# Output projection's weights and first heads loaded and split during attention's last phase

## The reference

```
hx = rms_norm(x, g_pre) * (1 + scale_x) + shift_x
q, k, v, gate = mla_qkv(hx, ...)                     # 8 heads, 192-wide q and k, 128-wide v
ox = softmax(q k^T / sqrt(192)) v                     # keys: 2048 latent + 256 context
yx = (ox * silu(gate)) @ w_o                          # 1024 x 1024, the output projection
x  = x + gate_x * rms_norm(yx, g_post)
```

## Time and profile before

| | us |
|---|---|
| three runs | 3099.14, 3100.43, 3102.71 |
| the profiled execution: its own time | 3098.24 |
| the profiled execution: span | 3096.4 |
| PE busy | 2925.2 (94% of the span) |
| DVE busy | 1815.5 (59%) |
| ACT busy | 1447.0 (47%) |
| POOL busy | 430.1 (14%) |
| mean granted clock of PE | 0.984 of full speed |

### The profile page before, as it was taken

How to read it: one execution, slowest core, us unless ns; L and a number is a source line. 1 busy time by engine, 2 the same in 40 slices (tenths; PEclk the granted TensorE clock), 3 DMA queues, 4 the chain that set the end, 5 groups by cost and what they waited for, 6 DMA issues and landing times. The chain is left out here.

```text
span 3096.4 us, 44414 instructions
## 1 busy us (share of the span) xinstructions
PE 2925.2 (94%) x14789; PEld 2437.0 (79%) x14789; DVE 1815.5 (59%) x3147; ACT 1447.0 (47%) x3071; POOL 430.1 (14%) x493
## 2 busy tenths in 40 slices
PE   2999999879999999999999999979899999999798
PEld 1877878758887887878788888868788888888687
DVE  6545545256777676766766777644344444445875
ACT  2644545345656565556556565534432221222553
POOL 1000000012221222122221222200001111112000
PEclk9999999989999999999999999989999999999899
DMA  6455464540111111121111110055342222222563
GB/s 219 161 186 197 160 214 139 178 126 31 47 57 57 57 47 47 42 73 42 51 44 58 57 42 25 11 188 187 144 134 78 71 73 69 71 77 76 175 196 131
DMA packets 222413, 312.31 MB, mean 101 GB/s; under 512 B 81376, under 2 KB 143088, under 8 KB 221040
## 3 DMA queue, kind: packets, MB, share of 16 engines
q1 hardware_dynamic: 217584, 301.18, 30.1%
q10 hardware_dynamic: 4608, 8.39, 0.7%
HBM read 211.85 MB, written 97.66 MB: 100 GB/s over the span
## 5 line engine op out<-in xcount | busy, mean ns | idle before, releaser
L1096 DVE TENSOR_TENSOR at_ptlo<-at_T,at_pthi 128x512 fp32r<-128x512 f32 x576 | 396.6, 689 | 325.6 <-ACT at_pthi L973 322.8
L957 ACT ACTIVATE at_prob<-at_S,at_nmax 128x512 f32<-128x512 f32 (+1 forms) x640 | 411.5, 659 | 370.7 <-DVE at_nmax L1071 366.9
L973 ACT ACTIVATE at_pthi<-at_T 128x512 fp32r<-128x512 f32 x576 | 349.6, 609 | 212.8 <-PE at_T L842 212.8
L1060 DVE TENSOR_REDUCE at_mx<-at_S 128x1 f32<-128x512 f32 (+1 forms) x640 | 393.3, 630 | 74.1 <-PE at_S L817 62.4
L842 PE MATMUL at_T<-ident,at_prob 128*128 128x128 f32 x2304 | 346.6, 273 | 1.7 <-DVE at_ptlo L1096 1.7
L842 PEld LDWEIGHTS at_T<-ident,at_prob 128*128 128x128 f32 x2304 | 279.5, 141 | 67.2 <-DVE at_ptlo L1096 11.0
L96 PE MATMUL ci_ps<-h1hi,ci_whi 128*128 128x512 f32 x768 | 300.0, 391 | 5.4 <-DVE h1lo L1780 5.4
L97 PE MATMUL ci_ps<-h1lo,ci_whi 128*128 128x512 f32 x768 | 299.5, 390 | 0.0
L98 PE MATMUL ci_ps<-h1hi,ci_wlo 128*128 128x512 f32 x768 | 299.3, 390 | 0.0
L812 PE MATMUL at_S<-at_khi,at_qhi 128*128 128x512 f32 (+1 forms) x640 | 250.0, 391 | 46.5 <-ACT at_prob L957 23.6
L96 PE MATMUL at_O<-at_pthi,at_vhi 128*128 128x512 f32 x576 | 270.5, 470 | 3.1 <-issue 2.4
(11 more groups left out here) (230 smaller groups left out, 6112.1 us busy)
## 6 DMA issues: line engine op xcount, KB each, us to landing
fr_w<-in_w_front SPq DMA_DIRECT2D x75, 512.0 KB, 4.1
at_wmod<-in_w_mod SPq DMA_DIRECT2D x32, 512.0 KB, 3.5
ci_w<-in_cv_w_in SPq DMA_DIRECT2D x24, 512.0 KB, 4.1
fr_w<-in_w_front SPq DMA_DIRECT2D x24, 384.0 KB, 3.9
values<-fr_ob SPq DMA_DIRECT2D x36, 256.0 KB, 2.8
at_kst<-k_nope SPq DMA_DIRECT2D x8, 1152.0 KB, 6.5
at_vst<-values SPq DMA_DIRECT2D x8, 1152.0 KB, 8.5
fr_x<-in_x SPq DMA_DIRECT2D x16, 512.0 KB, 7.5
```

Source lines behind the costliest of these rows:

```text
L957: nc.scalar.activation(prob[:, j % 2, i, k], S[:, c, 0:k.stop - k.start], ACT.Exp, scale=SCALE, bias=nmax[:, i % 2:i % 2 + 1], accum_out=l ...
L973: nc.scalar.activation(dst, T[:, (n + SLOTS * j) % 2], ACT.Copy).then_inc(s_hi, 1)
L1060: nc.vector.tensor_reduce(mx[:, i % 2, c:c + 1], S[:, c, 0:k.stop - k.start], AXX, ALU.max).then_inc(s_mx, 1)
L1096: nc.vector.tensor_tensor(ptlo[:, kt % 3], T[:, (n + SLOTS * j) % 2], pthi[:, kt % 3].bitcast(F32), ALU.subtract).then_inc(s_lo, 1)
```

## The change

Eight edits belong together.

1. The output projection's weights and the heads' pieces get fixed places in SBUF over tiles of attention that are spent by then (`placed` reserves an address). The high weights lie over `at_prob`'s first half, the raw weights over the staging and split keys and values, and the low part is written over the raw one in place. The same holds for the heads: `o_lo` and `o_raw` are one place.
2. SP issues the first four weight tiles in the last head's phase j = 1, and in the last phase the first piece of heads and the other four weight tiles, once all scores are made.
3. ACT copies 7 weight tiles and the first piece of heads in the last phase, after the copies of slots 1, 3, 5, 10, 12, 14, 16 and 7. DVE subtracts 4 weight tiles and the heads after slots 2, 5, 12, 15 and in "den" (slot 9).
4. `attn_out` starts with the copy of the eighth weight tile and the subtractions of the last four.
5. The stores of `at_og` and of the gate's rows are awaited where they are read: by SP ahead of `load_heads` and ahead of the load of `gp`. The waits at attention's end are gone.
6. As a piece is loaded over its own low part, piece p is loaded only when PE has finished piece p - 2, at tile 2p - 2, and is copied and subtracted at tile 2p - 1.
7. The wait ahead of the loads of the convolution's weights falls away, as they overlap nothing now.
8. The homes of the four blocks in `conv_in` change from (b + 1) % 4 to (0, 1, 3, 2); the order in which they are used does not.

```diff
+def load_heads(nc, net, sp, p):
+    sp.dma_start(net.o_raw[:, p % 2], net.og[:, :, p * NCOL:(p + 1) * NCOL].rearrange("k p n -> p k n")
+                 ).then_inc(net.s_o[p % 2], 16)
+def heads_high(nc, net, act, p):
+    act.wait_ge(net.s_o[p % 2], 16 * (p // 2 + 1))
+    nc.scalar.activation(net.o_hi[:, p % 2], net.o_raw[:, p % 2], ACT.Copy).then_inc(net.s_ohi, 1)
+def heads_low(nc, net, dve, p):
+    dve.wait_ge(net.s_ohi, p + 1)
+    nc.vector.tensor_tensor(net.o_lo[:, p % 2], net.o_raw[:, p % 2], net.o_hi[:, p % 2].bitcast(F32),
+                            ALU.subtract).then_inc(net.s_olo, 1)
+def w_o0_high(nc, net, act, k):
+    act.wait_ge(net.s_w0[k], 16)
+    nc.scalar.activation(net.w0hi[:, k], net.w0raw[:, k], ACT.Copy).then_inc(net.s_w0hi, 1)
+def w_o0_low(nc, net, dve, k):
+    dve.wait_ge(net.s_w0hi, k + 1)
+    nc.vector.tensor_tensor(net.w0lo[:, k], net.w0raw[:, k], net.w0hi[:, k].bitcast(F32),
+                            ALU.subtract).then_inc(net.s_w0lo, 1)
...
 def attention
+        W_HIGH, O_HIGH = {1: 0, 3: 1, 5: 2, 10: 3, 12: 4, 14: 5, 16: 6}, 7
+        W_LOW, O_LOW = {2: 0, 5: 1, 12: 2, 15: 3}, slots.index("den")
...
         @block.sync, phase(h, j, last)
+                if last and j == 1:
+                    sp.wait_ge(s_klo, HEADS * NCHUNK)
+                    sp.wait_ge(s_vlo, HEADS * VC)
+                    for k in range(KD // 2):
+                        sp.dma_start(net.w0raw[:, k], net.w_o0[:, k]).then_inc(net.s_w0[k], 16)
+                if last and j == NBH - 1:
+                    sp.wait_ge(s_qk, HEADS * NBH * QT * NCHUNK)
+                    sp.wait_ge(s_ogst[0], 16 * (HEADS * NBH // 2 - 1))
+                    load_heads(nc, net, sp, 0)
+                    for k in range(KD // 2, KD):
+                        sp.dma_start(net.w0raw[:, k], net.w_o0[:, k]).then_inc(net.s_w0[k], 16)
...
-            sp.dma_start(net.gp_row, gpT[:]).then_inc(s_rowst, 16)
-            sp.wait_ge(s_rowst, 16)
+            sp.dma_start(net.gp_row, gpT[:]).then_inc(net.s_rowst, 16)
...
             store_output(HEADS - 1, NBH - 1)
-            for k in range(2):
-                act.wait_ge(s_ogst[k], 16 * HEADS * NBH // 2)
...
 def attn_out
-            load_o(0)
-            for k in range(KD):
-                if k >= WR:
-                    sp.wait_ge(s_wlo, k - WR + 1)
-                sp.dma_start(wst[:, k % WR], net.w_o0[:, k]).then_inc(s_w[k % WR], 16)
-            load_o(1)
+            load_heads(nc, net, sp, 1)
+            sp.wait_ge(net.s_rowst, 16)
             sp.dma_start(gp[:], net.gp_flat[0:1, :].to_broadcast([P, D])).then_inc(s_gp, 16)
...
-                if n % TB == 0 and n // TB + 2 < NT // TB:
-                    sp.wait_ge(s_olo, n // TB + 1)
-                    load_o(n // TB + 2)
+                if n % TB == 0 and n and n // TB + 1 < NT // TB:
+                    p = n // TB + 1
+                    sp.wait_ge(s_y, n)
+                    j = p * W // BLK
+                    sp.wait_ge(net.s_ogst[j % 2], 16 * (HEADS * NBLK // 2 - (j < 2)))
+                    load_heads(nc, net, sp, p)
...
-            o_high(0)
-            for k in range(KD):
-                act.wait_ge(s_w[k % WR], 16 * (k // WR + 1))
-                nc.scalar.activation(whi[:, k], wst[:, k % WR], ACT.Copy).then_inc(s_whi, 1)
+            for k in range(W_HIGH, KD):
+                w_o0_high(nc, net, act, k)
+            heads_high(nc, net, act, 1)
             for n in range(NT):
-                if n % TB == 0 and n // TB + 1 < NT // TB:
-                    o_high(n // TB + 1)
+                if n % TB and n // TB and n // TB + 1 < NT // TB:
+                    heads_high(nc, net, act, n // TB + 1)
...
-            o_low(0)
-            for k in range(KD):
-                ...
+            for k in range(W_LOW, KD):
+                w_o0_low(nc, net, dve, k)
+            heads_low(nc, net, dve, 1)
             dve.wait_ge(s_gp, 16)
             for n in range(NT):
-                if n % TB == 0 and n // TB + 1 < NT // TB:
-                    o_low(n // TB + 1)
+                if n % TB and n // TB and n // TB + 1 < NT // TB:
+                    heads_low(nc, net, dve, n // TB + 1)
```

More of the change, by code:

```diff
@@ L973, in high @@
                 nc.scalar.activation(dst, T[:, (n + SLOTS * j) % 2], ACT.Copy).then_inc(s_hi, 1)
+                if isinstance(b, int) and b == HEADS * NBH - 1:
+                    if n == min(W_HIGH):
+                        act.wait_ge(s_tr, b * SLOTS)
+                    if n in W_HIGH:
+                        w_o0_high(nc, net, act, W_HIGH[n])
+                    if n == O_HIGH:
+                        heads_high(nc, net, act, 0)
             def store_output(h, j):
@@ L1092, in low @@
                 kt = slots[n]
[L1093 to L1097, removed]
+                if kt != "den":
+                    dve.wait_ge(s_hi, h * (SLOTS * NBH) + (n + SLOTS * j + 1))
+                    nc.vector.tensor_tensor(ptlo[:, kt % 3], T[:, (n + SLOTS * j) % 2], pthi[:, kt % 3].bitcast(F32),
+                                            ALU.subtract).then_inc(s_lo, 1)
+                if isinstance(h, int) and index(h, j) == HEADS * NBH - 1:
+                    if n in W_LOW:
+                        w_o0_low(nc, net, dve, W_LOW[n])
+                    if n == O_LOW:
+                        heads_low(nc, net, dve, 0)
             def output(h, j):
@@ L1337, in _ @@
         def _(act):
[L1338 to L1342, removed]
             def stat(n):
@@ L1484, in conv_in @@
         sb = lambda n, s, d=F32: st.enter_context(nc.sbuf_tensor("ci_" + n, s, d))
+        mine = 2 * NBLK * KD * BLK * 4 + 3 * NCOL * 4
+        sb("held", [P, mine // 4])
         wst = net.cw
@@ L1511, in home @@
         def home(b):
-            return (b + 1) % NBLK
+            return HOMES[b]
         def split_behind(n):
@@ L1932, in conv_out @@
         sb = lambda n, s, d=F32: st.enter_context(nc.sbuf_tensor("co_" + n, s, d))
-        z, wlo, gt, whi, vhi, vlo = (net.last[n] for n in ("z", "wlo", "gt", "whi", "vhi", "vlo"))
+        wlo, whi = (sb(n, [P, KD, D], F32R) for n in ("wlo", "whi"))
+        z, gt = sb("z", [P, 2, KD, W]), sb("gt", [P, 2, KD, W])
+        vhi, vlo = sb("vhi", [P, 2, KD, W], F32R), sb("vlo", [P, 2, KD, W], F32R)
+        sb("sums", [P, 3 * NCOL])
         wst = net.w1raw
@@ L2246, in build @@
         net.gpre, net.gpost = sb("g_pre", [P, 2, KD]), sb("g_post", [P, 2, KD])
[L2249 to L2253, removed]
[L2254 to L2263 removed]
+        held = NBLK * KD * BLK * 4
+        net.w0hi, net.w0lo, net.w0raw = (placed(nc, n, [P, KD, D], d, at) for n, d, at in (
+            ("w_o0_hi", F32R, 0), ("w_o0_lo", F32R, 73728), ("w_o0_raw", F32, 73728)))
+        net.o_hi, net.o_lo, net.o_raw = (placed(nc, n, [P, 2, KD, NCOL], d, at) for n, d, at in (
+            ("og_hi", F32R, 129024), ("og_lo", F32R, 145408), ("og_raw", F32, 145408)))
+        net.h1raw = placed(nc, "h1raw", [P, NBLK, KD, BLK], F32, 0)
+        net.cw = placed(nc, "cv_w", [P, 3, D], F32, CW_HOME)
+        net.w1raw = placed(nc, "w_o1_raw", [P, KD, D], F32, 0)
+        hlo, hhi = (placed(nc, n, [P, NBLK, KD, BLK], F32R, at) for n, at in (("h1lo", 0), ("h1hi", held)))
+        z0, zs, qs = (placed(nc, n, [P, NCOL], F32, 2 * held + i * 4 * NCOL)
+                      for i, n in enumerate(("z_first", "z_sum", "z_square_sum")))
         front(nc, net)
@@ L2266, in build @@
         attn_out(nc, net)
-        with ExitStack() as st:
-            st.enter_context(nc.sbuf_tensor("after_attention", [P, 2 * NBLK * KD * BLK + 3 * NCOL + 3 * D], F32))
-            conv_in(nc, net, hhi, hlo, z0, zs, qs)
-        with ExitStack() as st:
-            st.enter_context(nc.sbuf_tensor("after_convolution", [P, 2 * NBLK * KD * BLK + 3 * NCOL], F32))
-            conv_out(nc, net, z0, zs, qs)
+        conv_in(nc, net, hhi, hlo, z0, zs, qs)
+        conv_out(nc, net, z0, zs, qs)
 def constants():
```

73 lines of the change are left out of this document (28 added, 45 removed).

## The result

The changed kernel takes 3082.72 us (median of four runs, 3081.18 to 3084.72), the kernel before 3100.4 beside it: a ratio of 0.9942, 95% interval 0.9925 to 0.9960. That is faster by 17.7 us, where 14.1 were forecast. The profiled execution took 3082.16 us (span 3080.3), 16.1 less than the one of before. Lines have moved: the products are now lines 136 to 138, the weights' copy and subtraction lines 120 and 125, the heads' lines 109 and 114, the transposition of a slot line 897 and its subtraction line 1155, the gate product line 1255, the column's products lines 1262 to 1267 and the matmul on it line 927.

The account below looks back on a forecast made before the run. PE, busy 94% of the span, was taken as the bound, with time to win only where it idles or runs at half clock. 13.0 + 6.9 - 4.1 - 1.7 = 14.1 us gained: 3100.43 to 3086.3 us, range 3080.5 to 3092.

Parts of the forecast that it names:

- The gap: PE's idle time between attention and the output projection: 2.17 us instead of 15.17, 13.0 us gained.
- The first tile: The projection's first tile: 10.88 us instead of 17.78, 6.9 us gained, before 1.7 us taken off for half clock.
- likeness to 297.95 us: A similar PE gap at 297.95 us brought 3.4 us of half clock, so 1.7 us lost in the first tile.
- The bound of 2.4 us: Upper bound on the clock's loss in the first tile: half of the 4.8 us it had at half clock before.
- The last phase: Attention's last phase grows by the inserted copies and subtractions: 2.8 us, plus 1.3 for POOL, 4.1 us lost.
- the meeting with POOL: DVE's inserted subtractions and POOL's operations hold each other in attention's last phase: 1.3 us added, for the heads' subtraction.
- 3.6 had been named as a sign: Sign in attention's last phase: the heads' subtraction in "den" shows 3.6 us instead of 2.29.
- Its walk: Slot-by-slot reckoning of attention's last phase: PE 2.8 us late at the end; 6.6 with every hold against DVE.
- the first case: First weight subtraction meets POOL's chain: DVE first, POOL ends 1.2 us later; POOL first, DVE held up to 2.4 us.
- The steady state: The projection's later pieces of heads, each loaded one pair nearer its use: 1.0 us of slack, no cost, six times.
- heads become the wait: Rival: late heads stop PE at each of six projection pairs; slower, 3107 us, chance 0.03; milder, near 3097 us, 0.06.
- SP's queue and the rest: Early loads issued by SP in attention, the fallen wait ahead of the convolution's weights, the homes' new numbers: no cost.

Follow-up runs that it names:

- e1_await: The changed kernel with the two waits for the last stores put back at attention's end: 3085.08 us (one run).
- e5_fill: The changed kernel with five unread 128x512 matmuls between attention's last transposition and the block's end: 3081.14 us, ratio 0.9949 to the kernel before.
- e10_pool_small: The changed kernel with POOL's last-phase operations (diagonal's low part, modulation column product, gate product) cut to 8 columns each: 3083.76 us (one run).
- e3_column_late: The changed kernel with PE summing the last modulation column ahead of the last phase's last two slots instead of slot 8: 3081.00 us, ratio 0.9947 to before.
- e4_no_product: The changed kernel with POOL's chain on the modulation column taken out of the last phase (one small add instead): 3083.09 us (one run).
- e6_margin: The changed kernel with one more ACT copy ahead of each heads' copy in the projection's six odd tiles 3 to 13: 3087.28 us (one run).
- e2_loads_only: The changed kernel with weights and first heads still loaded in attention, but every copy and subtraction made in attn_out: 3084.99 us (one run).
- after_again: The changed kernel itself, unaltered, measured once more beside the kernel before: 3081.58 us, ratio 0.9952.
- e7_both: The changed kernel with the modulation column summed later and five spare matmuls behind attention's last transposition: 3080.03 us, ratio 0.9945 to the kernel before.
- e9_all: The changed kernel with last-phase subtractions in 128x512 pieces, the later modulation column and five spare matmuls together: 3080.90 us, ratio 0.9944 to the kernel before.

## Why the prediction came out right, step by step

- *The gap*: 13.0 us forecast, 12.71 measured. The block's end took 1.09 us, not 0.88, and PE began 0.20 us after SP's first issue, not 0.1. That it waits for no store is shown by e1_await (1.9 us otherwise).
- *The first tile*: 6.9 less 1.7, which is 5.2, forecast; 5.01 measured. That no weight tile is late is shown by e5_fill and e10_pool_small, with 11.2 us for the tile at full clock (why 0.3 over 10.88 is open). The clock's price is 1.57 us (e5_fill). The forecast by likeness to 297.95 us was right, but e10_pool_small shows that a gap of this length doesn't always bring the half clock. The bound of 2.4 us was misread: the first tile of before had a second stretch at half clock, after PE had stood still for 2.1 of 3.3 us, waiting for weight tiles:

```profile
2039.50:2042.80 3.30, 1.21 (x5) 1.00 0.99 344
2043.00:2046.00 3.00, 3.00 (x7) 0.50 1.10 375
```

- *The last phase*: 4.1 us forecast, 3.10 measured. This is the term that was mis-sized, in both of its parts. The splits cost 2.39 us, not 2.8 (e10_pool_small against before), and the meeting with POOL 0.71, not 1.3. The second also came by another way: not through the heads' subtraction (2.28 us and not held, where 3.6 had been named as a sign) but through the modulation column, which PE waited 1.45 us for. The prediction has that way in its text (POOL's chain ends 1.2 us later, and PE is late enough for about half of it; the second weight subtraction is held for at most 1 us, measured 0.75), but put nothing of it into the sum. Its walk has DVE first by 0.04 us in the first case, as at the diagonal here, and POOL first by 0.04 us at the gate product, where DVE was first by 0.60. What the walk left out there is what the hold of the second weight subtraction does to the order. Counted from the third slot's value products:

| | second subtraction | PE then waits | POOL at the gate product | DVE at the heads |
|---|---|---|---|---|
| changed | 1.97 us | 1.45 (column) | 10.89 | 10.29 |
| e3_column_late | 1.95 | 0.83 (DVE) | 10.09 | 9.59 |
| e4_no_product | 1.22 | 0 | 9.52 | 9.60 |
| e10_pool_small | 1.22 | 0 | 9.50 | 9.58 |

Where the subtraction is held, PE comes late to the products of "den", ACT copies them later, and POOL waits for that copy; DVE's own way leads through ACT's long copy of the heads and isn't put back by it. The column's wait then moves both. e4_no_product is the case that the walk described, and there the phase costs 25.57 us, 4.96 over before, as the half clock comes on top. So that the term is only 1.0 us off is in part luck: the order that it counts on didn't come, and would have cost more than it says.
- *The steady state*: nothing forecast, nothing measured (174.33 us both). The slack of 1.0 us is 0.9 by e6_margin, but at three pieces only; the other three have some 2.8 (an estimate, 1.0 and the 1.8 us by which the tile ahead of them is longer), so the rival "heads become the wait" had three pairs to stand at, not six.
- *SP's queue and the rest*: nothing forecast; e2_loads_only shows 20.63 us in the last phase with all loads early.

The three terms miss by -0.3, -0.2 and +1.0 us, 0.5 in sum. The medians differ by 3.1 us more than the stages show (17.7 - 14.6); 1.5 of that lie, in the profiled pair, outside the stages that the change touches, and the rest is within the spread of the runs; beside after_again the medians are 15.6 us apart. That the median came out 3.6 us below the forecast of 3086.3 therefore says nothing against the terms.

## What to carry to other kernels

A serial prologue (load, copy, subtract) ahead of a bound engine can be worth moving into the stage before even where that engine is full: here loads cost nothing there, and splits gave back 6.9 us for 3.1. Where an insert on DVE meets a chain on POOL, ask first who waits for either: POOL's gate product, held for 1.5 us, cost nothing, the wait of 1.45 us on an input of PE did, and taking load off one side can turn the order round and make it worse (25.57 for 23.71). When untouched stages wander by some us, compare fixed instructions, not medians.

## What the runs showed of the hardware

- An idle stretch of 2.46 us on PE was followed by some 3.4 us at 1.2 GHz in seven traces of eight, beginning between some 0.4 us before (e4_no_product) and 1.2 us after (e6_margin) PE's restart, and once not at all (e10_pool_small); 1.3 us never (three traces). Five products that nobody reads, in the idle time, save 1.57 us.
- What lies behind the sixteenth mean square is the same in the changed kernel and all its variants, and takes 868.4 to 871.7 us in their 13 traces (869.8 before). It is shortest in e5_fill and e7_both (868.5), but e9_all, with the same spare products, has 870.3: so that isn't their doing.
- In e6_margin a wait of 0.88 us on PE made a tile 1.21 us longer.
- A DVE subtraction and a POOL operation that both read two operands from SBUF hold each other, whichever is first: POOL 2.82 for 1.29 us when DVE was first by 0.60, DVE 3.35 for 2.28 us when POOL was first by 0.08.
